# Layer 0's gate modulation as row products beside the z tiles, with the remaining modulation quarters spread evenly over the FFN

## The reference, cut to what matters

```python
sc, scc = silu(c), silu(c_ctx)                     # vectors of 2048
for l in range(2):
    shift, scale, gate = split(sc @ w_ada[l] + b_ada[l], 3)        # w_ada[l]: 2048 x 6144
    shift_c, scale_c, gate_c = split(scc @ w_ada[l] + b_ada[l], 3)
    h  = rms(x,  norm_w[l]) * (1 + scale)   + shift
    hc = rms(xc, norm_w[l]) * (1 + scale_c) + shift_c
    qa, ka, va, qb, kb, vb, qc, kc, vc, z = project_stream(h, ...)  # and the same for hc
    x  = x  + gate   * ((attention outputs * silu(z))   @ w_out[l])
    xc = xc + gate_c * ((attention outputs * silu(z_c)) @ w_out[l]) # layer 0 only
```

## Time and profile before

| what | value |
|---|---|
| median of 3 runs | 3288.59 us (3288.5 to 3289.92) |
| the profiled execution | 3289.74 us |
| its span, first to last instruction | 3287.6 us |
| TensorE busy in the span | 3251.8 us, 99% |
| VectorE busy | 2240.7 us, 68% |
| ScalarE busy | 1431.3 us, 44% |
| share of TensorE in the chain that ended last | 94% |
| mean granted TensorE clock | 0.999 |

### The profile page before, as it was taken

One profiled execution on the slowest core, in us unless ns is written; L12 is line 12 of the kernel. 1 busy time (PEld: TensorE's weight loads), 2 busy tenths in 40 slices (PEclk: granted clock), 3 DMA queues, 4 the chain that ended last, 5 costly groups with the idle time before them and its releaser, 6 DMA issues.

```text
span 3287.6 us, 56246 instructions
## 1 busy us (share of the span) xinstructions
PE 3251.8 (99%) x20418; PEld 2783.6 (85%) x20418; DVE 2240.7 (68%) x3318; ACT 1431.3 (44%) x2193; POOL 614.2 (19%) x550
## 2 busy tenths in 40 slices
PE   8999999999999999999999999999999999999999
PEld 8999999998987777788888787777868888888978
DVE  7887877567877677677765566567657666774665
ACT  5444445444443343444543433532352363543353
POOL 4999930111440000000300000000001100000000
PEclk9999999999999999999999999999999999999999
DMA  6555555565567777777732222134326533322235
GB/s 219 185 180 183 185 184 185 186 212 182 203 232 253 282 265 279 255 273 263 273 108 101 72 88 78 58 109 148 108 80 214 204 132 111 137 90 96 94 107 171
DMA packets 159583, 557.67 MB, mean 170 GB/s; under 512 B 17520, under 2 KB 23808, under 8 KB 159232
## 3 DMA queue, kind: packets, MB, share of 16 engines
q1 hardware_dynamic: 154144, 534.67, 47.1%
q0 software_dynamic: 5216, 19.94, 1.8%
HBM read 548.23 MB, written 6.31 MB: 169 GB/s over the span
## 4 chain that ended last, share of the span: by engine, by line
PE 94%; DVE 3%; ACT 1%; issue 1%; DVEq 1%; ACTq 0%; DMA 0%; POOL 0%; SPq 0%
PE psum L2116 18%; PE psum L2120 18%; PE psum L2117 18%; PE psum L2143 15%; PE psum L2144 7%; PE psum L2327 4%; PE psum L2476 2%; PE psum L2502 2%; PE psum L2172 2%; PE psum L2487 2%; PE psum L2328 2%; DVE wlo L1309 1%; PE psum L2247 1%; PE psum L2433 1%; DVE rst L1340 0%
## 5 line engine op out<-in xcount | busy, mean ns | idle before, releaser
L844 ACT ACTIVATE whi<-raw 128x1024 fp32r<-128x1024 f32 (+3 forms) x844 | 864.8, 1030 | 1033.7 <-PE psum L2120 571.8
L1309 DVE TENSOR_TENSOR wlo<-raw,whi 128x1024 fp32r<-128x1024 f32 (+3 forms) x844 | 1035.5, 1233 | 398.6 <-ACT whi L844 370.5
L2116 PE MATMUL psum<-hcat,whi 128*128 128x256 f32 (+1 forms) x3436 | 1126.7, 328 | 7.1 <-DVE wlo L1309 6.4
L2120 PE MATMUL psum<-hcat,wlo 128*128 128x256 f32 (+1 forms) x3436 | 1110.6, 323 | 0.0
L2117 PE MATMUL psum<-hcat,whi 128*128 128x256 f32 (+1 forms) x3436 | 1110.4, 323 | 0.0
L2143 PE MATMUL psum<-hcat,whi 128*128 128x512 f32 x2048 | 727.1, 399 | 0.1
L2116 PEld LDWEIGHTS psum<-hcat,whi 128*128 128x128 f32 x3436 | 654.4, 190 | 75.7 <-issue 19.0
L2120 PEld LDWEIGHTS psum<-hcat,wlo 128*128 128x128 f32 x3436 | 654.3, 190 | 51.5
L2117 PEld LDWEIGHTS psum<-hcat,whi 128*128 128x128 f32 x3436 | 654.8, 191 | 49.2 <-issue 0.7
L2144 PE MATMUL psum<-hcat,wlo 128*128 128x256 f32 x2048 | 573.5, 280 | 0.0
L2143 PEld LDWEIGHTS psum<-hcat,whi 128*128 128x128 f32 x2048 | 384.5, 188 | 114.6 <-issue 25.6
(11 more groups left out here) (297 smaller groups left out, 3568.2 us busy)
## 6 DMA issues: line engine op xcount, KB each, us to landing
raw<-in_stream SPq DMA_DIRECT2D x978, 512.0 KB, 4.3
raw<-in_stream SPq DMA_DIRECT2D x18, 384.0 KB, 3.0
raw<-in_stream SPq DMA_DIRECT2D x24, 256.0 KB, 2.6
resid_dram<-X POOLq DMA_DIRECT2D x2, 2048.0 KB, 9.1
bias<-in_natten POOLq DMA_DIRECT2D x16, 256.0 KB, 3.0
X<-resid_dram POOLq DMA_DIRECT2D x4, 1024.0 KB, 6.1
raw<-in_stream SPq DMA_DIRECT2D x16, 192.0 KB, 2.4
crow<-c_dram POOLq DMA_DIRECT2D x3, 1024.0 KB, 7.3
```

The costliest lines, as they stand in the source:

```text
L844: act.activation(whi[:, c % HI_SLOTS, 0:n], raw[:, slot, 0:n], ACT.Copy).then_inc(hi_ready, 1)
L1309: vec.tensor_tensor(wlo[:, slot, 0:n], raw[:, slot, 0:n], whi[:, c % HI_SLOTS, 0:n].bitcast(F32), ALU.subtract).then_inc(lo_ready, 1)
L2116: pe.matmul(dst, h, cat[:, kk, c0:c0 + width], start=(q == 0 and k == 0), stop=False)
L2120: last = pe.matmul(dst, l_, cat[:, kk, c0:c0 + width], start=False, stop=(q == nq - 1 and k == nch - 1))
```

## The change

Layer 0's gate, 2048 outputs for `c` and `c_ctx`, is 32 row quarters. Before, 16 of them (8 chunks of 128 outputs) were row products and the other half of the gate was two blocks in the FFN. After, all 32 are row products: 8 beside the za tiles, 8 beside the zb tiles, 16 in stage c as before. The first 16 use the first half of the inputs, the 16 in stage c the second. In za and zb the products come behind `gated` and ahead of `norms`, in the slots `4t+1` and, for a tile's second quarter, `4t+2`; their unread output goes to the last two chunks of `X`. TensorE's z tiles wait for them at their last matmul, as the tiles of stage c do. The second load of `crow0` now follows the last product of zb.

The FFN keeps 128 quarters for 16 blocks: 24, 24, 24, 24, 32 in the five groups where 16, 32, 32, 32, 32 were. The core of the diff:

```diff
-MOD_GROUPS = [MOD_FEW if g == 0 else MOD_FFN for g in range(FF_GROUPS)]
+MOD_FEW = [0, 2] * 8 + [0] * LATE + [0, 2, 0, 0, 2, 0, 0, 2, 0, 2, 0, 0, 0]
+MOD_GROUPS = [MOD_FEW if g < FF_GROUPS - 1 else MOD_FFN for g in range(FF_GROUPS)]
...
-MOD_C = [1, 1, 2, 1, 2, 1, 2, 1, 2, 1, 2]
-C_WEAVE = weave([2] * 11, MOD_C)
-C_CHUNKS = sum(MOD_C) // 2
+ROW_MODS = dict(za0=[1, 1, 2, 1, 2, 1], zb0=[1] * 8, c0=[1, 1, 2, 1, 2, 1, 2, 1, 2, 1, 2])
+ROW_WEAVE = {name: weave([2] * len(m), m) for name, m in ROW_MODS.items()}
...
-    region("gate_mod", 3 * KD * 4)
+    region("gate_mod", 4 * KD * 4)
...
                 if t == 0:
+                    fence()
                     gains(0)
...
-            def gate0_products(e):
+            def gate0_products(name, e, out, some=slice(None)):
 
-                for pos, a in e["mods"]:
-                    s, (half_, t) = Q0["c0"] + pos, divmod(a, C_CHUNKS)
-                    j = 4 * C_BLOCK + t
+                for pos, a in e["mods"][some]:
+                    s, (half_, t) = Q0[name] + pos, divmod(ROWS0[name] + a, ROW_CHUNKS)
+                    j = ROW_OF[t]
                     vec.wait_ge(crow0_in, 16 * (half_ + 1))
                     vec.wait_ge(raw_in[s % SLOTS], 16 * (s // SLOTS + 1))
                     for c in range(2):
                         start = gate0_half[:, c, t:t + 1] if half_ else pv("b_ada", j)
                         total = ada_t[:, c, j:j + 1] if half_ else gate0_half[:, c, t:t + 1]
                         fence()
-                        last = vec.tensor_tensor_reduce(psum[:, 6:8, :].rearrange("p b c -> p (b c)"), raw[:, s % SLOTS, :],
+                        last = vec.tensor_tensor_reduce(out.rearrange("p b c -> p (b c)"), raw[:, s % SLOTS, :],
                                                         crow0[:, c, :], 1.0, start, ALU.mult, ALU.add, total)
                     last.then_inc(gate0_mods, 1)
...
                     if p is not None and p >= 2:
                         gated(us[p - 2])
+                    if name in ROW_WEAVE and s % 4 in (1, 2):
+                        gate0_products(name, ROW_WEAVE[name][s // 4], X[:, KD - 2:KD, :], slice(s % 4 - 1, s % 4))
                     if p is not None and p < len(us):
                         norms(us[p])
...
                         if rows and q == nq - 1 and k == nch - 1:
-                            pe.wait_ge(rows_made, rows[-1][1] + 1)
+                            pe.wait_ge(rows_made, made + rows[-1][1] + 1)
...
                 for t in range(Z_SPLIT[l]["ab".index(kind) + 1]):
+                    rows = ROW_WEAVE[name][t]["mods"] if name in ROW_WEAVE else ()
                     tile(C0[name] + 2 * t, 0, T0[name] + t, 0, hcat, 0, 2 * S, chunks_w(l),
-                         beside_=lambda h: slot(4 * t + h))
+                         beside_=lambda h: slot(4 * t + h), rows=rows, rows_made=gate0_mods, made=ROWS0.get(name, 0))
...
-                    pool.wait_ge(gate0_mods, C_CHUNKS)
+                    pool.wait_ge(gate0_mods, ROW_CHUNKS)
                     crow0_load(1)
```

More of the change, by code:

```diff
@@ L106, in weave @@
             pos, a = pos + 1, a + 1
-    assert a % 8 == 0
+    assert a % 4 == 0
     return out
@@ L120 @@
 Z_PAIRS = 4
-MOD_C = [1, 1, 2, 1, 2, 1, 2, 1, 2, 1, 2]
-C_WEAVE = weave([2] * 11, MOD_C)
-C_CHUNKS = sum(MOD_C) // 2
+ROW_MODS = dict(za0=[1, 1, 2, 1, 2, 1], zb0=[1] * 8, c0=[1, 1, 2, 1, 2, 1, 2, 1, 2, 1, 2])
+ROW_WEAVE = {name: weave([2] * len(m), m) for name, m in ROW_MODS.items()}
+ROWS0, _n = {}, 0
+for _name, _m in ROW_MODS.items():
+    ROWS0[_name] = _n
+    _n += sum(_m)
+ROW_CHUNKS = _n // 2
 MOD_OUT = [0] + [2, 2, 3, 2, 2, 3, 2, 2, 3, 2, 2, 3, 2, 2] + [0]
@@ L129, with row_mods @@
 FFN_AT = [3 * KD * g + 8 * FFN_BLOCK[g] for g in range(FF_GROUPS)]
-C_BLOCK = 3 * D // 512 - sum(MOD_C) // 8
-BLOCKS = [*range(C_BLOCK), *range(3 * D // 512, 5 * D // 512)]
+_blocks = range(5 * D // 512)
+ROW_BLOCKS = [*range(2 * D // 512, 3 * D // 512)] + [5 * D // 512 - 2, 5 * D // 512 - 1]
+ROW_BLOCKS = ROW_BLOCKS[4 - min(ROW_CHUNKS // 4, 4):ROW_CHUNKS // 4 if ROW_CHUNKS > 16 else 4]
+ROW_OF = [4 * b + i for b in ROW_BLOCKS for i in range(4)]
+BLOCKS = [b for b in _blocks if b not in ROW_BLOCKS]
+assert len(ROW_OF) == ROW_CHUNKS
 assert 8 * len(BLOCKS) == sum(map(sum, MOD_GROUPS)) and sum(MOD_OUT) == 2 * KD and not Z_BEFORE
+def row_mods(name):
+    return sum(ROW_MODS.get(name, ()))
 PHASES = [("conf", 32, 16), ("pool", 16, 8), ("sconv", 48, 24), ("mix", 2, 8),
@@ L139 @@
     _n = Z_SPLIT[_l]
-    PHASES += [(f"z{_l}", 2 * _n[0] + Z_MODS[_l], _n[0]), (f"a{_l}", 24, 12), (f"za{_l}", 2 * _n[1], _n[1]),
-               (f"b{_l}", 20, 10), (f"zb{_l}", 2 * _n[2], _n[2]), (f"c{_l}", 22 + (0 if _l else sum(MOD_C)), 11), (f"kvb{_l}", 12, 12),
+    PHASES += [(f"z{_l}", 2 * _n[0] + Z_MODS[_l], _n[0]), (f"a{_l}", 24, 12), (f"za{_l}", 2 * _n[1] + row_mods(f"za{_l}"), _n[1]),
+               (f"b{_l}", 20, 10), (f"zb{_l}", 2 * _n[2] + row_mods(f"zb{_l}"), _n[2]), (f"c{_l}", 22 + row_mods(f"c{_l}"), 11), (f"kvb{_l}", 12, 12),
                (f"qb{_l}", 9, 9), (f"out{_l}", 32 + (0 if _l else sum(MOD_OUT)), 16)]
@@ L185, in _converted @@
             own = {pos for e in Z_WEAVE[l] for pos, _ in e["pre"] + e["mods"]}
-        elif name in ("c0", "out0"):
-            own = {pos for e in (C_WEAVE if name == "c0" else OUT_WEAVE) for pos, _ in e["mods"]}
+        elif name in ROW_WEAVE or name == "out0":
+            own = {pos for e in ROW_WEAVE.get(name, OUT_WEAVE) for pos, _ in e["mods"]}
         of += [Q0[name] + k for k in range(nq) if k not in own]
@@ L2102, in weight, with tile @@
                 return whi[:, c % HI_SLOTS, col:col + n], wlo[:, SQ[c] % SLOTS, col:col + n]
-            def tile(s, d, ts, td, cat, c0, loff, width, nq=2, nch=8, k0=0, ready=None, beside_=None, rows=(), rows_made=None):
+            def tile(s, d, ts, td, cat, c0, loff, width, nq=2, nch=8, k0=0, ready=None, beside_=None, rows=(), rows_made=None, made=0):
                 pe.wait_ge(psum_free, FREE[ts] + td)
@@ L2413, in projected @@
                         cat_ready(JOBS_OF[f"cq{l}"][0])
-                    rows = C_WEAVE[u]["mods"] if name == "c" and l == 0 and u < len(C_WEAVE) else ()
+                    rows = ROW_WEAVE["c0"][u]["mods"] if name == "c" and l == 0 and u < len(ROW_WEAVE["c0"]) else ()
                     tile(SQ.index(s), 0, first + u, 0, cat, 0, 2 * S, w, nq=nq, nch=nch, k0=k0, ready=ready,
-                         rows=rows, rows_made=gate0_mods)
+                         rows=rows, rows_made=gate0_mods, made=ROWS0["c0"])
                 return items[len(tiles_):]
@@ L2862, in put_woven, with put_rows @@
                 put(mods[a_])
+    def put_rows(name, tiles_):
+        if name in ROW_WEAVE:
+            put_woven(ROW_WEAVE[name], tiles_, rows_c[ROWS0[name]:])
+        else:
+            put(tiles_)
     for g in range(-1, FF_GROUPS):
```

23 lines of the change are left out of this document (10 added, 13 removed).

## The result

The changed kernel takes 3293.0 us (median; 3292.0 to 3295.7) where the kernel before takes 3288.6 us (3287.4 to 3290.7) beside it: +4.45 us, a ratio of 1.0013 with a 95% interval of 1.0008 to 1.0019. Forecast were 3297.0 us, range 3281 to 3302, and a likeliest case (+8.4 us) whose own range, 3293 to 3301, holds the result only at its edge.

A forecast was written before the change was run, and what follows sets the result against it. TensorE was taken as the bound nearly everywhere. The FFN's -9.4 us, stalls in za and zb of +12.4 and clock falls of +5.4 summed to +8.4 us, so 3297.0 us, range 3281 to 3302.

The forecast's parts named there:

- likeliest case: Two clock falls, behind TensorE's long stalls at the ends of za tiles 2 and 4: +8.4 us in all, chance 0.42.

The follow-up runs named there:

- e5: Changed kernel with the second products of za slots 10 and 18 moved to stage c; 3283.8 us, ratio 0.9982 to the kernel before.
- e7: e6 with one za product (slot 9) and one zb product (slot 25) moved one slot earlier; 3280.0 us, ratio 0.9973 to the kernel before.
- e2: Changed kernel with the 16 products of za and zb reading only 512 of 1024 inputs; 3282.3 us, ratio 0.9979 to the kernel before.
- e3: Changed kernel with the product behind the norms instead of ahead, and one fence behind it; 3306.4 us, ratio 1.0056 to the kernel before.
- e1: Changed kernel with the 16 products of za and zb reading only 16 of 1024 inputs; 3280.1 us, ratio 0.997 to the kernel before.
- r3: The kernel before, unedited, executed and profiled once more; 3289.9 us.
- e4: Changed kernel with 14 unread matmuls ahead of each long wait at the ends of za tiles 2 and 4; 3290.1 us, ratio 1.0003.
- r1: The changed kernel, unedited, executed and profiled once more; 3297.1 us.
- e6: e5 with each product split in two, for c ahead of the norms and for c_ctx behind; 3282.2 us, ratio 0.9978 to the kernel before.

## What to carry to other kernels

Where two engines hand work to and fro, cost an added instruction at each handover separately, on both sides of it: how long could the other engine still have gone on, and who is queued behind the next step. Work at the end of a tile, where the next engine has one last instruction and nothing behind it, is the dearest place (10.9 of 12.5 us here for 2 of 8 products). Those two cost nothing in stage c (e5), and a product moved one slot to the side, to a slot without a pair, cost nothing either (e7). A wait of TensorE of 3 us and more mostly cost more than its length here: 3.70 and 3.26 us cost 4.2 us extra, while e2's 1.57 and 1.12 us cost little beyond themselves. The next section shows that length alone does not decide it.

## What the runs showed of the hardware

- **How long the clock stays down does not follow the length of the wait alone.** The lengths seen are 6.83 and 3.41 us: 3.70 us of waiting brought 6.83 and 3.26 brought 3.41 in za, three times each. In e3, waits of 5.19 and 4.85 us brought 6.83 each. The 3.26 us wait of layer 1 stands in all 12 executions: it brought 6.83 in three of them (the kernel before, e1, e2), 3.41 in eight (r3 among them), and none at all in e4:

```profile
2652.55 0.38 PE L2132 MATMUL psum<-hcat,whi 128*128 128x256 f32 x1 [3.25 <-DVE wlo L1322]
...
2650.00:2655.00 5.00, 2.45 (x20) 2.45 (x21) 4.39 (x7) 4.93 (x9) 0.00 (x0) 1.00 0.34 111
```

- **A shorter wait can do it too, where a longer one did not.** In e3 a single wait of 1.48 us, 21 us behind the one before it, is followed by a fall at 2099.65; the waits of 2.05 and 2.04 us in zb of the same execution are not followed by one, nor is the 1.57 us of e2. What else decides is open.

```profile
2098.12 0.70 PE L2493 MATMUL psum<-qkv 64*128 64x256 f32 x4 [1.48 <-ACT probs L1214]
...
2100.00:2105.00 5.00, 5.00 (x21) 3.98 (x19) 1.54 (x7) 3.73 (x9) 0.00 (x0) 0.69 0.12 48
```

- **The same wait falls in one execution and not in another.** Ahead of the FFN, TensorE waits 2.2 us for GpSimd in every kernel. In the stretch around it the granted clock is 1.00 in the kernel before (first row) and 0.72 in the changed one (second row), though no instruction there differs. Of the 12 executions 9 have this fall; both of the kernel before and e5 have not:

```profile
840.00:845.00 5.00, 2.78 (x23) 2.58 (x23) 3.04 (x8) 1.96 (x6) 1.74 (x3) 1.00 0.11 39
```

```profile
840.00:845.00 5.00, 2.77 (x14) 2.57 (x14) 2.73 (x8) 2.15 (x6) 1.94 (x3) 0.72 0.06 21
```

- **Two stretches of plain matmuls have two paces, at the same granted clock of 1.00.** The last 488 matmuls of the program take 86.2 us from start to start in six of the 12 executions (both of the kernel before, r1, e1, e5, e6) and 84.6 in the other six. The first row is the kernel before, the second the changed one; in 80 us the faster pace has 463 records for 455:

```profile
3200.00:3280.00 80.00, 80.00 (x455) 69.36 (x454) 49.71 (x59) 29.59 (x29) 0.89 (x1) 1.00 0.58 190
```

```profile
3205.00:3285.00 80.00, 80.00 (x463) 70.53 (x463) 49.69 (x59) 29.49 (x28) 0.89 (x1) 1.00 0.56 194
```

Between 714 and 807 us the same two matmul lines differ by 1.65 us between executions in the same way, and the kernel before has there the faster pace in its profiled execution and the slower one in r3. Why is open. Together with the falls above, these paces are most of the 3 us by which executions of one kernel differ, and the reason why the stages had to be compared between cuts.
